# An encoder block on one core: the first mixer's side work reordered, two 2 MB weight loads halved, and the first expert pair walked in another order

## The reference, cut to what matters

```python
def reference(x, ...):                              # x: (1, 512, 1024), float32
    h = rms_norm(x, norm1_g)
    z = h @ w_in                                    # 1024 -> 5120
    qa, ka, va, qb, kb, vb, ga, gb = split(z)
    ya = axial_gqa_attention(qa, ka, va) @ w_o_a    # mixer A: 8 heads of 64, 2 key/value heads
    yb = dilated_window_attention(qb, kb, vb) @ w_o_b   # mixer B: 12 heads in 3 groups
    x = x + (sigmoid(ga + b) * ya + sigmoid(gb + b) * yb) @ w_out
    h = rms_norm(x, norm2_g)
    aff = softmax(h @ w_router)                     # 16 experts, each takes its 64 best tokens
    for e in range(16):
        xin = h[idx[e]]                             # 64 x 1024
        a, u = xin @ w_gate[e], xin @ w_up[e]       # each matrix is 1024 x 1024, 4 MB
        y = (silu(a) * u) @ w_down[e] * g[e]
        x[idx[e]] += y
    return rms_norm(x, normf_g)
```

## Time and profile before

| | us |
|---|---|
| median of 3 runs | 868.34 |
| the profiled execution, by its own time | 867.77 |
| its span | 865.8 |
| TensorE busy | 842.6 (97%) |
| VectorE busy | 373.4 |
| ScalarE busy | 264.1 |

### The profile page before, as it was taken

The page is one execution under the profiler, slowest core; times in us unless marked ns, Lnnn a source line. Parts: engine busy times, 40 slices in busy tenths (PEclk is TensorE's granted clock), DMA queues, the critical chain, the costliest instruction groups (busy, mean ns, idle before and its releaser), DMA issues.

```text
span 865.8 us, 10447 instructions
## 1 busy us (share of the span) xinstructions
PE 842.6 (97%) x4229; PEld 513.7 (59%) x4229; DVE 373.4 (43%) x648; ACT 264.1 (31%) x461; POOL 29.0 (3%) x50
## 2 busy tenths in 40 slices
PE   9999999999999999999999999999999998989996
PEld 8898766787878888888534343344433433334332
DVE  5377977676616245427322236223231311321351
ACT  6233866685624234216011010010100101001231
POOL 1050000000000000003000000000000000000010
PEclk9999999999999999999999999999999999999999
DMA  9730112023034335884899999999999999999995
GB/s 286 175 98 1 49 49 98 24 72 104 27 122 131 95 87 146 305 372 163 333 410 418 425 426 430 424 428 428 424 431 428 427 430 425 430 427 428 429 410 236
DMA packets 81428, 239.20 MB, mean 276 GB/s; under 512 B 8039, under 2 KB 63463, under 8 KB 66789
## 3 DMA queue, kind: packets, MB, share of 16 engines
q1 hardware_dynamic: 75952, 235.94, 69.2%
q10 hardware_dynamic: 5284, 2.09, 1.0%
q0 software_dynamic: 144, 0.51, 0.1%
HBM read 235.92 MB, written 2.62 MB: 276 GB/s over the span
## 4 chain that ended last, share of the span: by engine, by line
PE 82%; DMA 12%; DVE 3%; ACT 1%; issue 1%; POOLq 0%; POOL 0%; SPq 0%; ACTq 0%; DVEq 0%
PE psum L1645 18%; PE psum L1158 11%; PE psum L1677 11%; PE psum L1159 11%; PE psum L1160 11%; DMA wslot<-in_w_down 7%; DMA wslot<-in_w_up 4%; PE psum L1602 3%; PE psum L1696 2%; PE psum L1345 2%; PE psum L1357 2%; PE psum L1805 2%; PE psum L1331 2%; PE psum L1315 1%; PE psum L1164 1%; PE psum L1610 1%
## 5 line engine op out<-in xcount | busy, mean ns | idle before, releaser
L1645 PE MATMUL psum<-wslot,xinT 128*64 128x512 f32 x1000 | 222.4, 595 | 5.8 <-DMA wslot<-in_w_up 3.8
L1645 PEld LDWEIGHTS psum<-wslot,xinT 128*64 128x64 f32 x1000 | 69.8, 137 | 143.5 <-issue 132.1
L1677 PE MATMUL psum<-wslot,actT 128*64 128x512 f32 x424 | 96.0, 597 | 5.0 <-DMA wslot<-in_w_down 5.0
L1158 PE MATMUL psum<-hT_hi,w_hi 128*128 128x512 f32 x208 | 82.9, 399 | 0.0
L1160 PE MATMUL psum<-hT_hi,w_lo 128*128 128x512 f32 x208 | 81.2, 390 | 0.0
L1159 PE MATMUL psum<-hT_lo,w_hi 128*128 128x512 f32 x208 | 81.2, 390 | 0.0
L1878 DVE TENSOR_TENSOR w_lo<-w_raw,w_hi 128x1024 fp32r<-128x1024 f32 (+1 forms) x46 | 52.9, 1174 | 44.8 <-ACT w_hi L795 44.7
L1677 PEld LDWEIGHTS psum<-wslot,actT 128*64 128x64 f32 x424 | 29.2, 137 | 61.4 <-issue 57.4
L1091 ACT ACTIVATE actT<-psum 128x512 f32<-128x512 f32 x16 | 9.6, 597 | 174.4 <-PE psum L1657 174.4
L2283 DVE TENSOR_TENSOR x<-x,psum 128x512 f32<-128x512 f32 x48 | 29.7, 681 | 57.8 <-PE psum L1696 57.8
L2273 DVE TENSOR_TENSOR y_lo<-psum,y_hi 64x512 fp32r<-64x512 f32 x28 | 19.3, 689 | 81.1 <-ACT y_hi L1101 80.7
(11 more groups left out here) (281 smaller groups left out, 1300.6 us busy)
## 6 DMA issues: line engine op xcount, KB each, us to landing
wslot<-in_w_up SPq DMA_DIRECT2D x27, 2048.0 KB, 25.3
wslot<-in_w_gate SPq DMA_DIRECT2D x25, 2048.0 KB, 26.7
wslot<-in_w_down SPq DMA_DIRECT2D x24, 2048.0 KB, 23.7
w_raw<-in_w_in SPq DMA_DIRECT2D x34, 512.0 KB, 4.3
wslot<-in_w_gate SPq DMA_DIRECT2D x12, 1024.0 KB, 9.5
wslot<-in_w_up SPq DMA_DIRECT2D x9, 1024.0 KB, 11.8
wslot<-in_w_down SPq DMA_DIRECT2D x9, 1024.0 KB, 7.7
w_raw<-in_w_out SPq DMA_DIRECT2D x8, 512.0 KB, 4.7
```

Of the source, the lines that this page charges most:

```text
L1158: pe.matmul(out_, s_hi, m_hi, start=(k == 0), stop=False)
L1645: mm = pe.matmul(bank[2 * e + n][CAP * f:CAP * f + CAP, :], xinT[:, HALF * h + k, CAP * e:CAP * e + CAP], wslot[place_of(m)][:, k % PART, ...
L1677: mm = pe.matmul(bank[4 + e][CAP * f:CAP * f + CAP, :], actT[:, e, k, CAP * h:CAP * h + CAP], wslot[place_of(m)][:, k % PART, SEQ * f:SEQ ...
```

## The change

- Mixer A: `A_LOWS` goes from (2, 6, 10, 16, 20, 26) to (7, 11, 17, 21, 26, 33), and ScalarE's halves of the same splits, which stood at turns 1 and 2 and behind reads of column groups, get a list of their own. Reads of the second half of a column group go one turn later; two value reads go one turn later; VectorE's `low_k(1)` goes from ahead of the loop to turn 2.
- Start: `split_lo(2)` goes ahead of `low_hT(3)`.
- Loads: half 15 and half 91 are loaded as two parts. Parts 20 to 31 are issued in the order 20 to 23, 27 to 30, 24, 25, 26, 31.
- Pair 0: the order of contractions is (expert 0, half 0), (1, 0), (0, 1), (1, 1). `gather(0, 1)` now stands behind the fourth step of expert 1, that is the twelfth of the pair, and `turn_xin(0, 1)` two steps later. `turn_pick` and `turn_act(0)` stand behind the fifteenth step of expert 1 (before: the seventh). The step numbers of `between` count both halves of one expert.
- Routing: VectorE's `add_residual(1, 3)` and `route_norm(0)` change places.

```diff
-FIRST_PARTED, LAST_PARTED = (*range(8, 15), 16), range(92, 96)
+FIRST_PARTED, LAST_PARTED = range(8, 17), range(91, 96)
...
-        O_READ, O_LOW = (10, 19, 26), (11, 21, NA)
-        A_LOWS = (2, 6, 10, 16, 20, 26)
+        O_READ, O_LOW = (10, 20, 26), (12, 22, NA)
+        A_HIGHS, A_LOWS = (5, 8, 13, 18, 23, 28), (7, 11, 17, 21, 26, NA + 1)
...
+        def col_read(g, hh):
+            if g == N_COL_A - 1:
+                return NA + 1
+            return filled_at(A_FILL, g) + 2 + hh * (1 if g == N_COL_A - 2 else 2)
...
-            for half in (*range(10, 16), 17, 18, 16, *range(19, len(HALVES) * PAIRS)):
+            for m in (20, 21, 22, 23, 27, 28, 29, 30, 24, 25, 26, 31):
+                load_part(m)
+            for half in (17, 18, 16, *range(19, len(HALVES) * PAIRS)):
                 load_half(half)
...
-                    if u == filled + 4 and g < 2 * KC // RING:
-                        split_hi(at[col_groups[g][1:]] + RING)
-                if u in (1, 2):
-                    split_hi(13 + u)
+                if u in A_HIGHS:
+                    split_hi(14 + A_HIGHS.index(u))
...
             def between_second_gates(p):
+                def first(step):
+                    if step == 3:
+                        gather(0, 1)
+                    if step == 5:
+                        turn_xin(0, 1)
+                    if step == 14:
+                        turn_pick(0, bank[4])
+                        turn_act(0)
...
-                gate_up(p, 0, between_gates(p))
-                gate_up(p, 1, between_second_gates(p))
+                for e, h in ((0, 0), (0, 1), (1, 0), (1, 1)) if p else ((0, 0), (1, 0), (0, 1), (1, 1)):
+                    gate_up(p, e, h, (between_gates, between_second_gates)[e](p))
...
             low_hT(2)
+            split_lo(2)
             low_hT(3)
...
             low_q(3)
-            low_k(1)
...
+                if u == 2:
+                    low_k(1)
                 if u in A_LOWS:
                     split_lo(14 + A_LOWS.index(u))
```

More of the change, by code:

```diff
@@ L925, in _ @@
                 for g in range(N_COL_A):
-                    filled = filled_at(A_FILL, g)
-                    if u == (filled + 2 if g < N_COL_A - 1 else NA + 1):
+                    if u == col_read(g, 0):
                         high_col(g, 0)
-                    if u == (filled + 3 if g < N_COL_A - 1 else NA + 1):
+                    if u == col_read(g, 1):
                         high_col(g, 1)
-                    if u == filled + 4 and g < 2 * KC // RING:
-                        split_hi(at[col_groups[g][1:]] + RING)
-                if u in (1, 2):
-                    split_hi(13 + u)
+                if u in A_HIGHS:
+                    split_hi(14 + A_HIGHS.index(u))
                 if u in O_READ:
@@ L1619, in turn_pick @@
                 t.then_inc(give_turned, 1)
[L1621 to L1651, removed]
@@ new lines, in gate_up @@
+            def gate_up(p, e, h, between):
+                if p or h:
+                    pe.wait_ge(xin_done, xin_count(p, h))
+                if h == 0 and p == PAIRS - 1 and e:
+                    pe.wait_ge(gf_done, 2)
+                if h == 0 and p:
+                    pe.wait_ge(actT_done, 2 * p - 1 + e)
+                    if e == 0:
+                        pe.wait_ge(slot_aff_done, 4 * (p + 1))
+                    else:
+                        pe.wait_ge(give_done, p + 1)
+                steps = [(n, k) for n in range(2) for k in range(HALF)]
+                if p == e == h == 0:
+                    steps.sort(key=lambda step: step[1] // PART)
+                for step, (n, k) in enumerate(steps):
+                    m = part_at(p, (w_gate, w_up)[n], h, e, k)
+                    if k % PART == 0:
+                        wait_part_in(pe, m)
+                    if p == e == h == 0 and k % PART == 0:
+                        pe.wait_ge(xin_done, k // PART + 1)
+                    for f in range(2):
+                        mm = pe.matmul(bank[2 * e + n][CAP * f:CAP * f + CAP, :],
+                                       xinT[:, HALF * h + k, CAP * e:CAP * e + CAP],
+                                       wslot[place_of(m)][:, k % PART, SEQ * f:SEQ * f + SEQ],
+                                       start=(h == 0 and k == 0), stop=(h == 1 and k == HALF - 1))
+                    if k % PART == PART - 1:
+                        mm.then_inc(w_slot_used[place_of(m)], 1)
+                    between(2 * HALF * h + step)
@@ L1715, in first @@
                         turn_first_xin(1)
[L1716 to L1719, removed]
                     if step == 9:
@@ L1759, in between_second_gates @@
             def between_second_gates(p):
+                def first(step):
[6 more added lines that the diff above has]
+                        turn_act(0)
                 def turn(step):
                     if step == 6:
-                        if 0 < p < PAIRS - 1:
+                        if p < PAIRS - 1:
                             scatter(p - 1, (0, 1) if p == 1 else (2, 3))
-                        if p == 0:
-                            turn_pick(0, bank[4])
                         turn_act(2 * p)
@@ L1769, in turn @@
                         scatter(0, (2, 3))
-                return turn
+                return turn if p else first
             def between_second_downs(p):
@@ L1888, in _ @@
             low_hT(2)
+            split_lo(2)
             low_hT(3)
-            for n in range(2, 6):
+            for n in range(3, 6):
                 split_lo(n)
@@ L2005, in _ @@
                 for g in range(N_COL_A):
-                    filled = filled_at(A_FILL, g)
-                    if u == (filled + 3 if g < N_COL_A - 1 else NA + 2):
+                    if u == col_read(g, 0) + 1:
                         low_col(g, 0)
-                    if u == (filled + 4 if g < N_COL_A - 1 else NA + 3):
+                    if u == (col_read(g, 1) + 1 if g < N_COL_A - 1 else NA + 3):
                         low_col(g, 1)
+                if u == 2:
+                    low_k(1)
                 if u in A_LOWS:
@@ L2150, in _ @@
             low_xn(0, 1)
+            add_residual(1, 3)
             route_norm(0)
-            add_residual(1, 3)
             low_xn(1, 0)
```

## The result

The changed kernel took 871.3 us (median; 869.56 to 874.63), the kernel before 868.59 us beside it (866.53 to 870.11). The ratio is 1.0041, 95% interval 1.003 to 1.0053: slower by 0.41%, some 3.6 us. My 869.0 had the sign of the small difference right and its size wrong, and the measured time lies just outside my range of 865.2 to 871.0. The profiled execution has a span of 869.2 us against 865.8.

A forecast was written before the change was run, and what follows sets the result against it. TensorE bounds the kernel to about 440 us, then a gapless weight stream whose start sets the end. Mixers with start +2.0, pair 0 -1.0, end -0.3 give +0.7 us on the median 868.34: 869.0 us, range 865.2 to 871.0.

The forecast's parts named there:

- Start, -0.3: Kernel start: one split moved into VectorE's idle time removes TensorE's 0.20 us wait; -0.3 us.
- Strip 14, +1.8: Mixer A, turn 5: TensorE's step 16 waits for strip 14's split, queued on VectorE behind the scores of 7; +1.8 us.
- Strip 16, +0.9: Mixer A, turn 16: TensorE's step 32 waits for strip 16's split, moved to VectorE's turn 17; +0.9 us.
- Relief, -0.4: Mixer A: of TensorE's 1.3 us of waits for probabilities, 0.9 us stay in the new order; -0.4 us.
- Mixers in sum: Start, split waits and relief together, reaching the routing in full: +2.0 us, bounds +0.7 and +2.8.
- Pair 0, -1.0: Weight stream at pair 0: places freed earlier give it a queue, putting it ahead at its twelfth part; -1.0 us.
- The first dip: Weight stream at 424 to 440 us: 363 in place of 430 GB/s, 2.5 us lost, put down to late freed places.
- my slower rival: Mixers cost +2.7 us and the stream's gain is given back by 475 us for lack of queue; 871.0 us, chance 0.14.
- Smaller loads: Halves 15 and 91 as 1 MB transfers: 0.2 us or less on four parts while a queue stands ahead.
- Last half, -0.3: Kernel end: TensorE 1.2 us earlier through the parted last up half, but the result's write then comes last; -0.3 us.

The follow-up runs named there:

- wait_filled_9: Changed kernel with 9 small unused matmuls put in front of TensorE's wait for strip 14; 869.84 us, 1.0027 against the kernel before.
- strip14_early: Changed kernel with strip 14's splits moved back, high part from turn 5 to 2, low part 7 to 3; 868.84 us, 1.0012 against the kernel before.
- pair_alone: Kernel before with only pair 0's new contraction order, the new load order and half 15 in two parts; 868.08 us, ratio 1.0002.
- pair_parts: `pair_alone` with halves 17 to 20 also loaded as two parts; 866.37 us, 0.9992 against the kernel before.
- mixer_alone: Kernel before with only mixer A's new order of splits and reads and `low_k(1)` in turn 2; 872.32 us, ratio 1.0059.
- last_alone: Kernel before with only half 91 loaded in two parts; 868.21 us, ratio 1.001.

## Why the prediction was wrong

- *Start, -0.3.* The wait of 0.20 us is gone in the trace, as forecast. Too small to be told in the changed kernel's time.
- *Strip 14, +1.8.* The mechanism was right, place and queue, and the wait a little larger, 2.16. **The step that failed stands here: "TensorE waits 2.5 - 0.7 = 1.8 us", and nothing more.** I priced a wait as its length. The rest also took the clock from 1.00 to 0.57 over the 4 us from 104 us on, 1.7 us, nearly as much again as the term itself. `wait_filled_9` shows this part by itself (1.55), `strip14_early` both together (3.37). The kernel before had no rest of this length ahead of the experts (its longest is 1.06 us) and so no row that warned of it.
- *Strip 16, +0.9.* Right, 0.9 in all five traces with this order. The clock behind it stays.
- *Relief, -0.4.* The waits for probabilities went in full (-1.3), and 0.57 us came in front of the third value product. Net -0.7, within my bounds.
- *Mixers in sum.* +2.0 forecast with the start, +4.1 to +4.3 measured, beyond my upper bound of 2.8. The bound was too low, since it bounded the lengths of waits alone.
- *Pair 0, -1.0.* The first dip filled as worked out, by 0.8 and 1.2 us. What failed was to stop at the twelfth part. The gain was given back by 480 us, at half 19 with its two places; this is what my slower rival said (stream has too little queue behind pair 0), and what I had against it, that the gather really leaves the early part, was true and beside the point. Of the 0.82 us that the changed kernel is shorter behind its first gate, 0.26 is the end's (below); some 0.5 I can't assign, and `pair_alone`, with the same pair 0, has +0.3 there; both are within what this stretch varies by, so I don't take it for a gain.
- *Smaller loads.* Right: 1 MB parts cost nothing that shows. `pair_parts` has eight of them more and runs at 423 GB/s through them; the figures of the Trainium skill (DMA: Bandwidth & Descriptors, section Bandwidth), which by my estimate from them would put 1 MB transfers 20% under 16 MB ones, are not seen where a queue stands ahead.
- *Last half, -0.3.* Right in the traces, by the mechanism named: 0.26 us, the write takes over. In the times it can't be seen (1.001, 0.9996 to 1.0024).

Put right, the sum is -0.3 + 2.16 + 0.9 - 0.7 + 1.7 + 0 - 0.3 = +3.5 us against +3.4 of span and +3.6 by the ratio. That it comes so near is in part chance: stretch by stretch the traces have 4.3 lost in mixer A, 0.3 more than the terms for it give, and 0.8 less behind the first gate, of which only 0.3 has a cause. Of the slower rival's 871.0 us, one half was right (the stream) and the other half right by size only: it reached +2.7 with waits, and the true way there was the clock.

## What to carry to other kernels

Price an added wait on TensorE by its length, and ask separately what clock it may cost behind it; look at the granted clock of the stretches that follow other waits of that length, in several traces, since one and the same kernel here lost it behind 2.16 us and kept it behind 2.63. Where no such wait is there, put that cost into the upper bound; here it was 1.7 us, and with it the bound of the mixers would have held what was measured. When work is moved later in a queue, count for each moved item which turn of the consumer asks for it, and whether what is ahead of it in the queue waits for the same event. And a gain in a stream of loads must be followed to the next place where the stream waits for the consumer; a load that needs two places is best cut so that each half waits for one.

## What the runs showed of the hardware

- A rest of TensorE of 2.16 us was followed by some 3.4 us at half clock, which began 1.5 us after it had restarted in the changed kernel and 0.6 us after in `mixer_alone` (granted 0.57 and 0.60 over 104 to 108 us). Small matmuls in place of the rest kept 1.00 in two kernels. Rests of 2.48 us (`last_alone`, near 764 us) and 2.63 us (the changed kernel, near 709) cost no clock. A rest of 1.06 us in the kernel before at 147 us, with 4 small transposes behind it, was followed by 1.00, as this window over the rest and the next one show:

```profile
144.00:150.00 6.00, 4.94 (x26) 3.08 (x26) 5.79 (x12) 4.36 (x10) 0.00 (x0) 1.00 0.72 254
150.00:154.00 4.00, 4.00 (x20) 1.79 (x17) 1.50 (x4) 1.18 (x3) 0.00 (x0) 1.00 0.48 143
```

- The Trainium skill (TensorE: Matmul & The Clock Gate, section Why this matters for your kernels) asks to keep TensorE free of long idle gaps between bursts of matmuls, since it goes back to half clock. The traces agree that a gap can do this (2.16 us, then 0.57), in a gap shorter than one would take from that section, and they hold a longer one (2.63 us) behind which the clock stayed at 1.00.
- A matmul of 128 columns by the identity in float32 takes 0.22 us from start to start (20 in 4.4 us), so nine of them filled 2.0 us.
- TensorE's pace in the first 14 us differs between executions of the same code: the four matmuls shown took 2.17 or 3.78 us, and the first strip matmul came up to 2.7 us later for it.
- A load into two places went out when the later one was free. Cut in two, its first part went 1.7 us earlier, and 12 us of the stream ran at 423 in place of 372 GB/s.
- The write of the result behind the last weights lands 13.7 to 14.8 us after its issue in the thirteen traces; 13.7 in the kernel before and 13.8 in `last_alone`, where TensorE ended earlier against the stream.
